# A sample group's attention queries: broadcast by matmul in PSUM against broadcast by DMA in SBUF, in a two-layer decoder step

## The chip, the cores and the metric

One Trainium2 chip, 8 cores, all with the same program on different data: each core holds one of the 8 prompt sequences and 16 of the 128 samples. The metric is the device time of the slowest core in microseconds.

## The reference, cut to what matters

```python
def mem_attend(u, k, v, w_q, w_o):
    b, t, d = u.shape
    q = jnp.einsum('btd,de->bte', u, w_q).reshape(b, t, MEM_HEADS, MEM_HEAD_DIM)
    s = jnp.einsum('bthd,bnhd->bhtn', q, k).astype(jnp.float32) * (MEM_HEAD_DIM ** -0.5)
    p = jax.nn.softmax(s, axis=-1).astype(v.dtype)
    o = jnp.einsum('bhtn,bnhd->bthd', p, v).reshape(b, t, d)
    return jnp.einsum('btd,de->bte', o, w_o)

for i in range(DEPTH):                      # DEPTH = 2; D_MODEL = 1024
    x = x + mixer_i(rmsnorm(x, g_mix[i]))   # 0: causal pooling, 1: gated short convolution
    x = x + mem_attend(rmsnorm(x, g_attn[i]), mem_k[i], mem_v[i], w_q[i], w_o[i])
    x = x + sq_relu_mlp(rmsnorm(x, g_ffn[i]), w_up[i], w_down[i])
```

The prompt group (8 sequences of 2048 tokens) attends to 256 memory tokens whose K and V are computed here. The sample group (128 samples of one new token) attends to cached K and V, 256 tokens for each sample and layer, which are read from DRAM: 1 MB of K and 1 MB of V for each sample and layer in fp32.

## The kernel before, in words

**Tiles.** A core has 2048 prompt tokens and 16 sample tokens, in five tiles of 416, 416, 416, 416 and 400 columns; the last holds 384 prompt tokens and the 16 samples. The residual `X` is kept transposed (8 chunks of 128 features by 2064 tokens, fp32) in SBUF for the whole program; `U3` beside it holds the normalised input in bf16 and then the attention output.

**Stages.** The pooling mixer (to about 100 us), attention and MLP of layer 0, the convolution mixer (from about 840 to 1030 us), attention and MLP of layer 1. `layer` is called once for each layer with the last two.

**Attention.** `layer` goes through the tiles in the order `seq = [0, 4, 1, 2, 3]`; step k is the tile `seq[k]`. Q for the first tile is made ahead (8 groups of 8 matmuls, each group in one PSUM bank, evacuated by ScalarE). In each step four heads follow one another. A head h consists of `S(k, h + 1)` (scores of the next head: 4 matmuls, two banks, exponentiated by ScalarE into `PT`), a share of the list `big`, `PVh(k, h)` (6 matmuls, three banks: the denominators, which ScalarE turns into reciprocals, and two outputs, which VectorE multiplies by them and writes into `U3` at L316) and a second share of `big`. `big` holds the Q groups of the next tile and the O groups of an earlier one (`Ogroup`: 8 matmuls that read all 8 chunks of the tile's `U3`, one bank, added to `X` by VectorE). The table `cut` says how many eighths of `big` come where. `norm_h` squares half a tile on ScalarE; `norm_t` sums the squares with 8 matmuls and writes the normalised tile with 8 VectorE operations (L312), in head 2 of each step.

**Samples.** While the prompt tiles go on, one sample after the other is attended to in 18 slots. A slot i does four things: `SE(i - 1)`, the exponential of the scores of sample i - 1 on ScalarE and its copy into the zero-padded `PZ`; `SB(i - 2)`, 4 matmuls of 512 columns with V, which accumulate in bank 7; `SDV(i)`, the two loads of V on POOL's queue; `SQB(i)`, two matmuls of 512 columns whose left operand selects row i of `QS`, so that q of sample i stands on all 128 partitions in banks 5 and 6; and `SA(i)`, in which VectorE multiplies the two K tiles with it, 8 operations of 256 columns with a running sum (L336), each followed by a read of the accumulator. Each half of `SA` is followed by `SDK`, which loads a K tile (512 KB) on SP's queue into the buffer that this half released; there are three K buffers, so the tile of the second half of sample i + 1 is issued in the middle of sample i. `sample_q(1)` makes `QS` (16 partitions by 1024, bf16) at the end of head 2 of step 0: 8 transposes of the last tile's Q (L292) and a ScalarE copy (L328). The slots stand in the list `slots` for the first 12 samples; one is among the O groups of the last tile, and the other five stand in the first MLP stages (`mid`).

**Order and waits.** There is no scheduler: each engine runs its instructions in program order, and `Prog.add` derives the semaphores from the byte ranges of reads and writes. `PSv` marks a whole bank, and as exclusive (`excl=True`): a read of a bank is tracked as a write, so two reads of a bank by one engine other than TensorE are ordered by a semaphore too. `nxt()` hands out PSUM banks in turn, `bank_ctr % bank_mod`; `bank_mod` is 5 during attention and the first MLP stages, since banks 5 and 6 hold the sample's q and bank 7 its output, and 8 later. `wrelease_spread` cuts the load that replaces `wq` into 8 pieces, of which `wspread_step(2)` issues two in each slot on POOL's queue.

**Lines.** L283 is the matmul helper, L287 and L292 those for transposes and mixed groups, L300 and L303 activations, L312 `scalar_tensor_tensor`, L316 `tensor_tensor`, L328 and L330 copies on ScalarE and VectorE, L336 the multiply with a sum, L343 every DMA.

Of the kernel before, what the change touches and what calls it, by code (L numbers as in the profile page):

```python
# [8 lines left out]
BF16 = mybir.dt.bfloat16  # L9
# [4 lines left out]
PE, ACT, DVE, POOL, SP = "pe", "act", "dve", "pool", "sp"  # L14
NCORES = 8
D = 1024
NCH = 8
SEQ = 2048
NS = 16
# [4 lines left out]
QDB = 1 << 28  # L24
# [108 lines left out]
def build_program():  # L133
    nc = bass.Bass("TRN2", target_bir_lowering=False)
# [34 lines left out]
    ncs_d = dout("ncs", [NS, 2, D])  # L169

    mn_d = nc.dram_tensor("mn", [128, NCH, NMEM], BF16, kind="Internal").ap()

    es = contextlib.ExitStack()
    MEM = es.enter_context(nc.sbuf_tensor("MEM", [128, MEM_BYTES // 2], BF16))
# [2 lines left out]
    def DV(ap):  # L177
        return V(ap, [])
# [53 lines left out]
    def sl(a, b):  # L232
        return slice(a, b)

    def PSv(bank, a, b, m=128):
        return V(PS[0:m, bank, a:b], [(PSB + bank * 2048, PSB + (bank + 1) * 2048)], excl=True)
# [6 lines left out]
    bank_mod = [7]  # L243

    def nxt():
        b = bank_ctr[0] % bank_mod[0]
        bank_ctr[0] += 1
        return b
# [3 lines left out]
    def palloc(dt, shape):  # L252
        t = T(top[0], dt, shape)
        top[0] += (t.nbytes + 63) // 64 * 64
        return t
# [12 lines left out]
    IDB = palloc(BF16, [128])  # L268
# [13 lines left out]
    def mm(out, lhsT, rhs, start, stop):  # L282
        P.add(PE, "c", lambda e, o=out.ap, l=lhsT.ap, r=rhs.ap: e.matmul(out=o, lhsT=l, rhs=r, start=start, stop=stop),  # L283
              [lhsT, rhs], [out])
# [9 lines left out]
    def act(out, in_, func, scale=1.0, bias=0.0):  # L294
        rd = [in_]
        sc = scale
        if isinstance(scale, V):
            rd.append(scale)
            sc = scale.ap
        P.add(ACT, "c", lambda e, o=out.ap, i=in_.ap: e.activation(out=o, in_=i, func=func, bias=bias, scale=sc), rd, [out])  # L300
# [25 lines left out]
    def cp(out, in_, eng=DVE):  # L326
        if eng == ACT:
            P.add(ACT, "c", lambda e, o=out.ap, i=in_.ap: e.copy(out=o, in_=i), [in_], [out])  # L328
        else:
            P.add(eng, "c", lambda e, o=out.ap, i=in_.ap: e.tensor_copy(out=o, in_=i), [in_], [out])  # L330
# [4 lines left out]
    def ttr(out, in0, in1, acc):  # L335
        P.add(DVE, "c", lambda e, o=out.ap, a=in0.ap, b=in1.ap, c=acc.ap: e.scalar_tensor_tensor(  # L336
            out=o, in0=a, scalar=1.0, in1=b, op0=ALU.mult, op1=ALU.mult, accum_out=c), [in0, in1], [out, acc])
# [4 lines left out]
    def dma(q, out, in_, chan, after=()):  # L342
        P.add(q, "d", lambda e, o=out.ap, i=in_.ap: e.dma_start(out=o, in_=i), [in_], [out], chan=chan, after=after)  # L343
# [485 lines left out]

    def layer(l, side=None, tail=None):  # L830
        fin = l == 1
        bank_mod[0] = 5
        s2 = Scratch2()
        SQ = s2.alloc(BF16, [NCH, TW])
        HB = [s2.alloc(BF16, [NCH, TW]) for _ in range(2)]
# [7 lines left out]
        assert so == ZOFF  # L843
        KS = [s2.alloc(F32, [D]) for _ in range(3)]
        VS = [s2.alloc(BF16, [2, 512]) for _ in range(4)]
        QS = s2.alloc(BF16, [D])
        PZ = [s2.alloc(BF16, [4, PZW]) for _ in range(2)]
        OSN = T(KS[0].off, F32, [512])
        Wq, Wo = W(f"wq{l}"), W(f"wo{l}")
        seq = [0, 4, 1, 2, 3]  # L850
# [3 lines left out]
        def norm_h(ti, half):  # L854
            c0, n, npmt, ns = TILES[ti]
            act(SQ(sl(half * 4, half * 4 + 4), sl(0, n)), X(sl(half * 4, half * 4 + 4), sl(c0, c0 + n)), AF.Square)
# [13 lines left out]
        def Ogroup(ti, ec):  # L870
            c0, n, npmt, ns = TILES[ti]
            bk = nxt()
            for kc in range(NCH):
                mm(PSv(bk, 0, n), Wo(kc, sl(ec * 128, (ec + 1) * 128)), U3(kc, sl(c0, c0 + n)), kc == 0, kc == NCH - 1)
            tt(X(ec, sl(c0, c0 + n)), PSv(bk, 0, n), X(ec, sl(c0, c0 + n)), ALU.add)
# [26 lines left out]
        def sample_q(k):  # L902
            npmt = TILES[seq[k]][2]
            bk = nxt()
            psb = PS[0:NS, bk, :].bitcast(BF16)
            iv = PSv(bk, 0, 1).ivs
            for c in range(NCH):
                tp(V(psb[:, c * 128:(c + 1) * 128], iv, True), HB[k % 2](c, sl(npmt, npmt + NS)), IDB())
            cp(QS(p=(0, NS)), V(psb, iv, True), eng=ACT)

        def SDK(i):
            if i < 2 * NS:
                dma(SP, KS[i % 3](), DV(ck_d[l, i // 2, (i % 2) * 128:(i % 2 + 1) * 128, :]), f"ks{i % 3}")

        def SQB(b):
            sel = V(IDB.ap[0:NS, b:b + 1].broadcast_to([NS, 128]), IDB(sl(b, b + 1)).ivs)
            for hf in range(2):
                mm(PSv(5 + hf, 0, 512), sel, QS(sl(hf * 512, (hf + 1) * 512), p=(0, NS)), True, True)

        def SDV(b):  # L920
            for hf in range(2):
# [3 lines left out]
        def SA(b):  # L925
            for ncx in range(2):
                ks = KS[(2 * b + ncx) % 3]
                for h in range(4):
                    a = sl(h * 256, (h + 1) * 256)
                    ttr(ks(a), ks(a), PSv(5 + h // 2, (h % 2) * 256, (h % 2 + 1) * 256),  # L930
                        SS(b, ncx * 2 + h // 2, sl(h % 2, h % 2 + 1)))
                SDK(2 * b + ncx + 3)

        def SE(b):
            act(PBC(sl(0, 4), sl(2 * b, 2 * b + 2)), SS(b), AF.Exp, scale=1.0 / 16.0)
# [11 lines left out]
        def slot():  # L947
            i = sctr[0]
            sctr[0] += 1
            if 0 <= i - 1 < NS:  # L950
                SE(i - 1)
            if 0 <= i - 2 < NS:
                SB(i - 2)
            if i < NS:
                SDV(i)
                SQB(i)
                SA(i)
            wspread_step(2)

# [25 lines left out]
        for ec in range(NCH):  # L985
            Qgroup(0, ec)
            if ec == 3:
                norm_t(seq[1], R_ATTN + l)
        slots = [(0, 3), (1, 0), (1, 1), (1, 3), (2, 0), (2, 2), (3, 0), (3, 1), (3, 3), (4, 0), (4, 1), (4, 3)]
        for k in range(5):  # L990
            big = []
            if k + 1 < 5:
                big += [lambda ec=ec: Qgroup(k + 1, ec) for ec in range(NCH)]
            if k > 0 and seq[k - 1] != 4:
                big += [lambda ec=ec: Ogroup(seq[k - 1], ec) for ec in range(NCH)]
            nb = len(big)
            cut = [0, 1, 2, 3, 4, 5, 6, 7, 8] if k else [0, 2, 4, 6, 7, 8, 8, 8, 8]
            nrm = (seq[k + 2], R_ATTN + l) if k + 2 < 5 else ((k - 3, R_FFN + l))
            S(k, 0)
            for h in range(4):  # L1000
                if h < 3:
                    S(k, h + 1)
                if h < 2:
                    norm_h(nrm[0], h)
                for f in big[nb * cut[2 * h] // 8: nb * cut[2 * h + 1] // 8]:
                    f()
                PVh(k, h)
                if h == 2:
                    norm_t(*nrm)
                for f in big[nb * cut[2 * h + 1] // 8: nb * cut[2 * h + 2] // 8]:  # L1010
                    f()
                if (k, h) == (0, 2):
                    sample_q(1)
                if (k, h) in slots:
                    slot()
            if k == 3:
                wrelease_spread(f"wq{l}")
# [295 lines left out]
```

How the kernel before makes its waits and increments, by code:

```python
    def emit(name, e):  # L1202
        known = {}
        for op in P.q[name]:
            for d in op.cwaits:
                key = ("e", d.eng)
                if known.get(key, 0) < d.val:
                    e.wait_ge(sems[d.eng], d.val)
                    known[key] = d.val
            for ch, val in op.dwaits:
                key = ("c", ch)
                if known.get(key, 0) < val:
                    e.wait_ge(chans[ch], val)
                    known[key] = val
            ins = op.fn(e)
            if op.kind == "d":
                ins.then_inc(chans[op.chan], 16)
            elif op.sig:
                ins.then_inc(sems[name], 1)
        if name == SP:
            for ch, cnt in P.chan_count.items():
                if known.get(("c", ch), 0) < cnt * 16:
                    e.wait_ge(chans[ch], cnt * 16)
```

## Time and profile before

| | before |
|---|---|
| three runs, median | 1682.01 us (1681.29 to 1682.10) |
| the profiled execution, its own time | 1683.78 us |
| its span, slowest core (core 7) | 1682.0 us |
| spans of the eight cores | 1675.8 to 1682.0 us |
| TensorE busy | 1625.3 us (97%) |
| VectorE, ScalarE, POOL busy | 886.9, 515.8 and 83.3 us |
| K loads of the samples, 64 of 512 KB, median to landing | 6.7 us |
| V loads of the samples, 64 of 256 KB, median to landing | 6.9 us |
| attention of layer 0, of layer 1 | about 115 to 285 us, 1020 to 1190 us |

In the profile a busy time counts the union of an engine's instructions, and matmuls overlap with the next one, so that the mean duration of one is longer than the time from one start to the next. The idle time before an instruction is put down to what it waited for last. PEld is the weight load, which overlaps the matmuls.

### The profile page before, as it was taken

The page shows a single profiled execution, that of the slowest core. Times are in us where ns is not written, and L with a number is a line of the kernel's source. Part 1 is how long each engine was busy: PE and PEld are TensorE (multiplying, and loading weights), DVE is VectorE, ACT ScalarE, POOL GpSimd, SP SyncE. Part 2 cuts the span into 40 slices and gives each one's busy share as a digit, 9 for nine tenths or more (in the row PEclk, how much of TensorE's full clock was granted, in tenths as well). Part 3 has the DMA queues.
Part 4 walks back from the last instruction along what each step waited for, and adds up shares of the span by engine and source line. Part 5 has one row for each costly group of instructions (what it writes and reads, how often), then busy time and mean ns, then how long its engine had stood idle before and what let it go on. Part 6 is the DMA issues. An engine that isn't in the chain of part 4 may idle for free.

```text
span 1682.0 us, 27775 instructions; the slowest of 8 cores (1675.8 to 1682.0 us)
## 1 busy us (share of the span) xinstructions
PE 1625.3 (97%) x9556; PEld 918.4 (55%) x9556; DVE 886.9 (53%) x1979; ACT 515.8 (31%) x996; POOL 83.3 (5%) x120
## 2 busy tenths in 40 slices
PE   5899999999999999999999999999999999999997
PEld 4754454555555555555555554544555555555565
DVE  4655667644433444455666573657654444444455
ACT  4765442312112211222222136443312111111244
POOL 1010011100000000000000000101100000000000
PEclk8999999999999999999999999999999999999999
DMA  9995658617506333306000067556813503303013
GB/s 243 195 180 100 141 106 177 106 35 114 87 13 112 65 67 51 51 2 100 1 1 1 1 94 140 120 138 134 168 26 55 86 12 51 51 1 51 10 74 120
DMA packets 68835, 137.97 MB, mean 82 GB/s; under 512 B 3918, under 2 KB 27598, under 8 KB 68684
## 3 DMA queue, kind: packets, MB, share of 16 engines
q0 software_dynamic: 50304, 76.44, 31.1%
q1 hardware_dynamic: 18396, 59.77, 10.4%
q8 instruction: 80, 1.31, 0.3%
q14 instruction: 55, 0.45, 0.1%
HBM read 199.25 MB, written 14.36 MB: 127 GB/s over the span
## 4 chain that ended last, share of the span: by engine, by line
PE 90%; DVE 3%; DMA 3%; ACT 2%; issue 1%; SPq 1%; DVEq 0%; ACTq 0%
PE PS L283 88%; DVE MEM L312 2%; DMA MEM<-ck 2%; PE PS L292 1%; DMA MEM<-mem 1%; PE PS L287 1%; ACT MEM L303 1%; SPq L343 1%; ACT MEM L300 1%; DVE MEM L336 1%; DVE MEM L316 0%; ACT MEM L328 0%; ACT PS L300 0%; DVE MEM L330 0%; DVEq L1208 0%
## 5 line engine op out<-in xcount | busy, mean ns | idle before, releaser
L283 PE MATMUL PS<-MEM 128*128 128x416 bf16 (+7 forms) x8900 | 1570.8, 338 | 47.2 <-DVE MEM L316 20.6
L283 PEld LDWEIGHTS PS<-MEM 128*128 128x128 bf16 (+4 forms) x8900 | 860.0, 99 | 746.5 <-issue 103.5
L316 DVE TENSOR_TENSOR MEM<-PS,MEM 128x416 f32<-128x416 f32 (+5 forms) x601 | 339.1, 583 | 330.4 <-PE PS L283 269.1
L300 ACT ACTIVATE MEM<-PS 128x416 f32<-128x416 f32 (+3 forms) x465 | 234.4, 515 | 654.9 <-PE PS L283 552.4
L316 DVE TENSOR_TENSOR MEM<-MEM 128x416 bf16<-128x416 f32 (+1 forms) x320 | 186.5, 588 | 256.7 <-ACT MEM L300 256.7
L312 DVE SCALAR_TENSOR_TENSOR MEM<-MEM 128x416 bf16<-128x416 f32 (+5 forms) x314 | 191.8, 659 | 100.4 <-ACT MEM L300 95.3
L300 ACT ACTIVATE MEM<-MEM 128x1 f32<-128x1 f32 (+7 forms) x201 | 125.1, 632 | 95.1 <-DVE MEM L316 77.5
L336 DVE SCALAR_TENSOR_TENSOR MEM<-MEM,PS 128x256 f32<-128x256 f32 x256 | 100.6, 419 | 33.6 <-DMA MEM<-ck 10.9
L328 ACT COPY MEM<-PS 128x512 f32<-128x512 f32 (+4 forms) x76 | 41.4, 547 | 177.1 <-PE PS L283 155.2
L328 ACT CAST MEM<-PS 128x416 bf16<-128x416 f32 (+3 forms) x101 | 51.8, 516 | 61.3 <-PE PS L283 53.0
L300 ACT ACTIVATE PS<-PS 128x416 f32<-128x416 f32 (+2 forms) x65 | 32.8, 504 | 122.0 <-PE PS L283 122.0
L343 POOL DMA_DIRECT2D MEM<-cv x64 | 45.0, 709 | 283.2 <-PE PS L283 282.8
L312 DVE SCALAR_TENSOR_TENSOR MEM<-PS,MEM 128x1024 f32<-128x1024 f32 (+2 forms) x20 | 25.6, 1281 | 26.0 <-ACT MEM L300 26.0
L287 PE MATMUL PS<-MEM 128*128 128x128 bf16 (+1 forms) x384 | 34.6, 249 | 1.1 <-issue 0.5
L292 PE MATMUL PS<-MEM 128*128 128x128 f32 (+8 forms) x272 | 33.7, 266 | 0.6 <-DVE MEM L312 0.5
L343 POOL DMA_DIRECT2D MEM<-w_down x22 | 14.0, 634 | 399.1 <-PE PS L283 347.5
L287 PEld LDWEIGHTS PS<-MEM 128*128 128x128 bf16 (+1 forms) x384 | 31.8, 119 | 1.6 <-issue 1.1
L292 PEld LDWEIGHTS PS<-MEM 128*128 128x128 f32 (+8 forms) x272 | 28.5, 131 | 7.4 <-issue 3.9
L303 ACT ACTIVATE MEM<-PS 128x1024 bf16<-128x1024 f32 (+2 forms) x20 | 20.4, 1018 | 34.5 <-PE PS L292 34.5
L303 ACT ACTIVATE MEM<-MEM 128x1024 bf16<-128x1024 f32 (+1 forms) x19 | 20.0, 1054 | 13.0 <-DMA MEM<-x 7.6
L330 DVE COPY MEM<-MEM 128x2 f32<-128x2 f32 (+2 forms) x120 | 16.1, 168 | 15.0 <-ACT MEM L300 14.8
L336 DVE DVE_READ_ACCUMULATOR MEM<-MEM,PS 128x1 f32 x256 | 21.2, 83 | 0.0
(26 smaller groups left out, 83.1 us busy)
## 6 DMA issues: line engine op xcount, KB each, us to landing
MEM<-ck SPq DMA_DIRECT2D x64, 512.0 KB, 6.7
MEM<-w_up POOLq DMA_DIRECT2D x8, 2048.0 KB, 16.5
MEM<-cv POOLq DMA_DIRECT2D x64, 256.0 KB, 6.9
MEM<-w_down POOLq DMA_DIRECT2D x6, 2048.0 KB, 16.3
MEM<-x SPq DMA_DIRECT2D x16, 512.0 KB, 14.3
y<-MEM SPq DMA_DIRECT2D x15, 512.0 KB, 2.6
MEM<-w_conv_in POOLq DMA_DIRECT2D x3, 2048.0 KB, 16.2
MEM<-w_kv POOLq DMA_DIRECT2D x4, 1024.0 KB, 25.0
```

Source lines behind the costliest of these rows:

```text
L283: P.add(PE, "c", lambda e, o=out.ap, l=lhsT.ap, r=rhs.ap: e.matmul(out=o, lhsT=l, rhs=r, start=start, stop=stop), [lhsT, rhs], [out])
L287: P.add(PE, "c", lambda e, o=out.ap, l=lhsT.ap, r=rhs.ap: e.matmul(out=o, lhsT=l, rhs=r, start=start, stop=stop, is_transpose=is_transpose ...
L292: P.add(PE, "c", lambda e, o=out.ap, i=in_.ap, d=ident.ap: e.transpose(out=o, in_=i, identity=d), [in_, ident], [out])
L300: P.add(ACT, "c", lambda e, o=out.ap, i=in_.ap: e.activation(out=o, in_=i, func=func, bias=bias, scale=sc), rd, [out])
L303: P.add(ACT, "c", lambda e, o=out.ap, i=in_.ap, c=acc.ap: e.activation(out=o, in_=i, func=func, bias=0.0, scale=1.0, accum_out=c), [in_], ...
L312: P.add(eng, "c", lambda e, o=out.ap, a=in0.ap, b=in1.ap: e.scalar_tensor_tensor(out=o, in0=a, scalar=sc, in1=b, op0=op0, op1=op1), rd, [out])
L316: P.add(eng, "c", lambda e, o=out.ap, a=in0.ap, b=in1.ap: e.tensor_tensor(out=o, in0=a, in1=b, op=op), [in0, in1], [out])
L328: P.add(ACT, "c", lambda e, o=out.ap, i=in_.ap: e.copy(out=o, in_=i), [in_], [out])
L330: P.add(eng, "c", lambda e, o=out.ap, i=in_.ap: e.tensor_copy(out=o, in_=i), [in_], [out])
L336: P.add(DVE, "c", lambda e, o=out.ap, a=in0.ap, b=in1.ap, c=acc.ap: e.scalar_tensor_tensor(out=o, in0=a, scalar=1.0, in1=b, op0=ALU.mult, ...
L343: P.add(q, "d", lambda e, o=out.ap, i=in_.ap: e.dma_start(out=o, in_=i), [in_], [out], chan=chan, after=after)
```

## The change

1. `SQB` is gone. `sample_q` writes `QS` to a DRAM tensor `qd`, and `SDQ(b)` reads row b of it back, broadcast to 128 partitions, into one of two SBUF buffers `QB` (bf16, 2 KB a partition; `QS` is the first of them). `SDQ(0)` and `SDQ(1)` follow the store, `SDQ(b + 2)` follows `SA(b)`. All of them are on SP's queue. `SA` multiplies with `QB` instead of banks 5 and 6.
2. `bank_mod` is 7 in `layer` instead of 5.
3. The O groups: before, all 8 of the previous tile stood behind the Q groups in steps 1, 3 and 4. Now four or eight stand ahead of the Q groups in every step: tile 0 in steps 1 and 2, tile 1 in steps 3 and 4, tile 2 in step 4, which has 12.
4. Four slots move, so that steps 1 to 4 have 3, 3, 3 and 2 samples instead of 3, 2, 3 and 3. In step 4 the two halves of the squares are made in heads 0 and 2 and `norm_t` comes in head 3.

```diff
-        bank_mod[0] = 5
+        bank_mod[0] = 7
...
-        QS = s2.alloc(BF16, [D])
+        QB = [s2.alloc(BF16, [D]) for _ in range(2)]
+        QS = QB[0]
...
             cp(QS(p=(0, NS)), V(psb, iv, True), eng=ACT)
+            dma(SP, V(qd_d[l], [(QDB + 8192 + l * 4096, QDB + 12288 + l * 4096)]), QS(p=(0, NS)), "qd")
+            for b in range(2):
+                SDQ(b)
...
-        def SQB(b):
-            sel = V(IDB.ap[0:NS, b:b + 1].broadcast_to([NS, 128]), IDB(sl(b, b + 1)).ivs)
-            for hf in range(2):
-                mm(PSv(5 + hf, 0, 512), sel, QS(sl(hf * 512, (hf + 1) * 512), p=(0, NS)), True, True)
+        def SDQ(b):
+            if b < NS:
+                dma(SP, QB[b % 2](), V(qd_d[l, b:b + 1, :].broadcast_to([128, D]),
+                                       [(QDB + 8192 + l * 4096, QDB + 12288 + l * 4096)]), f"qb{b % 2}")
...
-                    ttr(ks(a), ks(a), PSv(5 + h // 2, (h % 2) * 256, (h % 2 + 1) * 256),
+                    ttr(ks(a), ks(a), QB[b % 2](a),
                         SS(b, ncx * 2 + h // 2, sl(h % 2, h % 2 + 1)))
                 SDK(2 * b + ncx + 3)
+            SDQ(b + 2)
...
-                SQB(i)
                 SA(i)
...
-        slots = [(0, 3), (1, 0), (1, 1), (1, 3), (2, 0), (2, 2), (3, 0), (3, 1), (3, 3), (4, 0), (4, 1), (4, 3)]
+        slots = [(0, 3), (1, 0), (1, 2), (1, 3), (2, 1), (2, 2), (2, 3), (3, 1), (3, 2), (3, 3), (4, 1), (4, 2)]
...
-            if k > 0 and seq[k - 1] != 4:
-                big += [lambda ec=ec: Ogroup(seq[k - 1], ec) for ec in range(NCH)]
+            og = [[], [(0, 0)], [(0, 4)], [(1, 0)], [(1, 4), (2, 0), (2, 4)]][k]
+            big = [lambda t=t, ec=ec: Ogroup(t, ec) for t, e0 in og for ec in range(e0, e0 + 4)] + big
...
-                if h < 2:
-                    norm_h(nrm[0], h)
+                if h in ((0, 2) if k == 4 else (0, 1)):
+                    norm_h(nrm[0], h // 2 if k == 4 else h)
...
-                if h == 2:
+                if h == (3 if k == 4 else 2):
                     norm_t(*nrm)
```

## Rows read from the trace of the kernel before

**Rows 1.** The page, part 1: busy time, share of the span, instructions.

```profile
PE 1625.3 (97%) x9556; PEld 918.4 (55%) x9556; DVE 886.9 (53%) x1979; ACT 515.8 (31%) x996; POOL 83.3 (5%) x120
```

**Rows 2.** All cores: span and mean granted clock of TensorE.

```profile
core 1: 1675.8 us, clock 0.991
...
core 7: 1682.0 us, clock 0.987
```

**Rows 3.** Waits of TensorE, 100 to 330 us: total, times, longest.

```profile
PE PS L283 <- DVE MEM L316: 11.1, 6, 4.2
PE PS L283 <- ACT MEM L328: 0.5, 1, 0.5
```

**Rows 4.** The same, 1000 to 1240 us.

```profile
PE PS L283 <- DVE MEM L316: 9.5, 6, 2.7
```

**Rows 5.** Windows, core 7: length, busy by engine, then PEclk, DMA share, GB/s.

```profile
145.00:150.00 5.00, 5.00 (x22) 2.49 (x21) 2.13 (x12) 2.72 (x5) 0.00 (x0) 0.71 0.55 143
205.00:210.00 5.00, 3.62 (x13) 1.65 (x14) 1.62 (x6) 2.50 (x3) 0.00 (x0) 0.66 0.84 210
265.00:270.00 5.00, 4.62 (x14) 2.05 (x15) 5.00 (x10) 0.00 (x0) 1.73 (x3) 0.50 0.92 179
270.00:275.00 5.00, 5.00 (x25) 2.23 (x23) 3.54 (x9) 2.60 (x4) 0.14 (x1) 0.92 0.96 140
1045.00:1050.00 5.00, 5.00 (x21) 2.43 (x20) 2.74 (x14) 2.81 (x5) 0.00 (x0) 0.66 0.40 114
1105.00:1110.00 5.00, 3.38 (x11) 1.44 (x12) 1.86 (x8) 2.46 (x3) 0.00 (x0) 0.71 0.67 211
1165.00:1170.00 5.00, 5.00 (x21) 2.30 (x18) 5.00 (x10) 0.37 (x1) 0.54 (x1) 0.66 1.03 183
```

**Rows 6.** The same view of core 1, behind its wait at 204 us.

```profile
205.00:210.00 5.00, 5.00 (x31) 2.77 (x29) 0.56 (x2) 3.78 (x6) 0.00 (x0) 1.00 0.31 106
```

**Rows 7.** Groups by form, TensorE, 500 to 600 us (MLP): count, busy us, mean ns.

```profile
L283 PE MATMUL PS<-MEM 128*128 128x416 bf16 x391 | 70.2, 339 | 0.0
...
L283 PE MATMUL PS<-MEM 128*128 128x512 bf16 x40 | 9.4, 379 | 0.0
```

**Rows 8.** Timeline, 138 to 144 us: start, length, what, [idle before, releaser].

```profile
138.08 0.98 ACT L328 COPY MEM<-PS 16x1024 bf16<-16x1024 bf16 x1
138.36 4.59 DVE L312 SCALAR_TENSOR_TENSOR MEM<-MEM 128x416 bf16<-128x416 f32 x8 [0.99 <-ACT MEM L300]
...
139.21 1.67 PE L283 MATMUL PS<-MEM 16*128 16x512 bf16 x8 [0.53 <-ACT MEM L328]
...
142.87 1.08 DVE L316 TENSOR_TENSOR MEM<-PS,MEM 128x416 bf16<-128x416 f32 x2
...
143.59 16.66 PE L283 MATMUL PS<-MEM 128*128 128x384 bf16 x83 [2.71 <-DVE MEM L316]
```

**Rows 9.** The same view, inside a sample's multiplies at 296 us.

```profile
296.68 0.42 DVE L336 SCALAR_TENSOR_TENSOR MEM<-MEM,PS 128x256 f32<-128x256 f32 x1
...
297.03 0.42 DVE L336 SCALAR_TENSOR_TENSOR MEM<-MEM,PS 128x256 f32<-128x256 f32 x1
...
297.56 0.42 DVE L336 SCALAR_TENSOR_TENSOR MEM<-MEM,PS 128x256 f32<-128x256 f32 x1
```

**Rows 10.** The same view, a multiply in step 4 that waits for K.

```profile
262.89 0.42 DVE L336 SCALAR_TENSOR_TENSOR MEM<-MEM,PS 128x256 f32<-128x256 f32 x1 [4.10 <-DMA MEM<-ck]
```

**Rows 11.** DMA, 245 to 275 us: a queue's packets, MB, share; an issue's median landing.

```profile
q1 hardware_dynamic: 864, 3.15, 29.4%
...
MEM<-ck SPq DMA_DIRECT2D x6, 512.0 KB, 7.2
```

**Rows 12.** DMA issues of the whole span: KB each, median us to landing.

```profile
MEM<-gv SPq DMA_DIRECT2D x1, 512.0 KB, 3.7
...
ys<-MEM SPq DMA_DIRECT2D x1, 64.0 KB, 1.9
npp<-MEM SPq DMA_DIRECT2D x1, 60.0 KB, 6.3
```

More of the change, by code:

```diff
@@ L171, in build_program @@
     mn_d = nc.dram_tensor("mn", [128, NCH, NMEM], BF16, kind="Internal").ap()
+    qd_d = nc.dram_tensor("qd", [2, NS, D], BF16, kind="Internal").ap()
     es = contextlib.ExitStack()
```

## The prediction, made before the change was run

> **What bounds the kernel now.** I read the page first. TensorE is busy 1625.3 of 1682.0 us [rows 1], so the time can only fall if TensorE gets less to do, idles less, or runs at a higher clock. The list of cores [rows 2] says which of these varies: core 1 ends 6.2 us before core 7 and was granted 0.991 against 0.987 of the full clock. The waits of TensorE give the places: in layer 0's attention stage it waits 11.1 us for VectorE's evacuations (L316) in six waits and 0.5 us for one ScalarE copy [rows 3]; in layer 1's, 9.5 us in six [rows 4], and the same 0.5 us. The MLP, the longest part, has none. Then the windows of 5 us: behind the long waits the granted clock is 0.50 to 0.71 in five-microsecond windows in which TensorE is mostly busy [rows 5], so each long wait is paid a second time at the lower of its two levels (1.2 against 2.4 GHz). What that costs is (1 - clock) x 5 us: 1.45 + 1.7 + 2.5 + 0.4 in layer 0, 1.7 + 1.45 + 1.7 in layer 1, that is 6.05 and 4.85 us. On core 1 the stretch behind the wait at 204 us stayed at 1.00 [rows 6], which is why the cores differ.
>
> So what TensorE loses around attention on core 7 is 11.6 + 6.05 = 17.65 us in layer 0 and 10.0 + 4.85 = 14.85 us in layer 1. ScalarE, POOL and the queues matter here only through VectorE.
>
> **Part 1, the selector matmuls go.** SQB issued two 512-column matmuls for each of 16 samples in 2 layers: 64. They ran in TensorE's stream and nothing covers them. In the MLP 391 matmuls of 416 columns take 70.2 us, 0.180 each, which is 0.221 for 512 columns; the 512-column ones there take 9.4/40 = 0.235 [rows 7]. I take 0.22: **14.1 us** (ends 14.1 and 15.0). The 0.53 us wait of the first SQB for the copy of q [rows 8] goes too; it is among the stalls.
>
> **Part 2, VectorE's sample work gets shorter.** SA is 8 multiplies with a sum. Their starts are 0.35 us apart where the bank of q changes and 0.53 apart where two read the same bank [rows 9]: the program marks a read of a bank as exclusive, so the second waits for the first on VectorE's own semaphore. q in SBUF has no such mark, so I take 0.35 for all: 2.8 us a sample instead of 3.5. Below, 2.8 may be too dear by nothing that a row shows; above, it stays 3.5. This lies beside matmuls, so it is worth nothing in itself; it shortens what the banks must bridge.
>
> **Part 3, seven banks and spread O groups.** An allocation returns to the same bank after 7 instead of 5. With the costs of [rows 7], a group is 8 x 0.18 = 1.44 us and a head's scores and PV 10 x 0.18 = 1.8 us. A head with three groups takes 8 banks in 6.1 us (7.0 with a sample's four V matmuls), so 7 banks let TensorE run some 5.5 us ahead; 5 banks at four groups a head gave about 4. The longest VectorE block is one norm, 8 operations in 4.59 us, then two of 0.54 [rows 8], often with SA behind it. VectorE's work in tile step 1, 2 or 3 of the change: 3 samples x 3.0 + 4 O evacuations x 0.59 + 4 x 1.08 + 4.59 = 20.3 us, against TensorE's 12 x 1.44 + 4 x 1.8 + 3 x 0.94 = 27.3. In step 4: 2 x 3.0 + 12 x 0.59 + 4.32 + 4.59 = 22.0 against 17.3 + 7.2 + 1.9 = 26.4. Before, step 4 had three samples and eight O groups: 3 x 3.7 + 4.7 + 4.32 + 4.59 = 24.7 against 11.5 + 7.2 + 2.8 + 1.3 = 22.8, VectorE-bound; the 4.17 us wait there is this, with a K tile that came 4.10 us late [rows 10]. And step 4's norm now stands behind the last head's PV, so that its 8 statistics matmuls and two groups (4.3 us) lie between that head and the O groups of tile 3 that read it. I take all waits from step 1's end on as gone, but 1.0 us a layer for what I can't see.
>
> **What stays: the passage from step 0 to step 1.** It is late for another reason. VectorE does the norm from 138.36 to 142.95 and then the two PV evacuations of head 3, until 143.95; TensorE stood still 2.71 us for their bank [rows 8]. After the change TensorE does S(1,0), S(1,1) without the 0.53 + 0.44 us of SQB, until 138.7 + 2 x 0.65 = 140.0. Then comes not a Q group but O(0,0), which reads the very U3 chunks 6 and 7 that these evacuations write. It gets through six of eight matmuls, to 141.1, and waits until 143.9: 2.8 us. So the stall stays about as long; only the work done before it is larger. I take 2.8 us and one clock dip of 1.7 (the 0.66 windows of [rows 5]) in each layer. What stays in a layer is 2.8 + 1.7 + 1.0 = 5.5 us.
>
> **Part 4, the new transfers.** q goes from SBUF to DRAM and back to 128 partitions before SA(0) can start. The copy of q ends at 139.06; VectorE is free for SA(0) at 143.95, so 4.9 us are covered by the norm. Two legs, on a DMA that is nearly idle just then: a 64 KB store landed in 1.9 us and a broadcast row of 512 KB in 3.7 [rows 12]; here it is 32 KB and 256 KB, so 1.9 + 3.7 = 5.6 us at most by these, 3.8 if the second leg is like the first. I take 0 to 0.7 us late and count 0, as O(0,0)'s bank isn't wanted again for 4 us. The other end is the 6.3 us of the early npp store [rows 12] for each leg: 12.6, so 7.7 us late in each layer. If the cover were gone it would be the whole trip. [...] SP waits meanwhile for the copy and the store; behind it stand only the first two rows and the refill of K, which waits for SA(0) anyway.
>
> For all other samples the row is issued a whole sample ahead, behind the K tiles that SP issues for the same release, so SP waits for nothing new. Each is 128 packets of 2 KB. A packet on that queue costs 0.294 x 16 x 30 / 864 = 0.163 us [rows 11] at 3.6 KB, so a row takes 0.7 (by bytes) to 1.3 us (by packets) of all 16 engines, hidden unless it delays K. There is the danger: a K tile lands in 7.2 us in the crowded stretch [rows 11], and neighbouring samples are now 7.0 us apart in six pairs a layer (9 before with four groups a head). So VectorE will wait 1 to 1.5 us for K there; it has 4 to 7 us of slack in a step and TensorE 5.5 us of banks. I price it at the 1.0 us above. POOL's own order is as before but for the weight pieces (two a slot): step 4 issues four instead of six, the slot among tile 3's O groups two as before, and the rest goes out behind those groups; they are first read two MLP halves of 8 x 1.44 us later, 23 us against a landing of some 6 to 9 us, so I price that at nothing. The second q buffer moves PZ up by 2 KB, which changes only which early tile its clearing waits for: nothing.
>
> **The sum.** 14.1 + (17.65 - 5.5) + (14.85 - 5.5) = 35.6 us off the profiled execution's 1683.8 us (span 1682.0) gives 1648.2. The three runs' median, 1682.0, is 1.8 below that execution, so I forecast **1646.4 us**. About 0.2% (3.4 us) is what a measurement of this kernel can tell from no change.
>
> **Rivals.**
> 1. *Cleaner than I think*: the stall at step 1 brings no dip, as on core 1 [rows 6], and nothing else stays: 2 x 2.7 us more, 1641. For it: the K slack. Against: the slowest of eight cores counts, and core 7 had a dip behind every wait of 2.6 us or more.
> 2. *K tiles late.* With the rows' traffic K lands 3 us or more too late in one or two pairs a layer, as it did at 262.89 [rows 10]. One such costs 2.7 us of stall and a dip of 1.7; two a layer, 4 x 4.4 = 17.6: 1664. For it: samples in neighbouring heads of steps 2 and 3, DMA share 0.92 to 1.03 in the windows at 265 and 1165 [rows 5]. Against: the wq0 successor's pieces no longer meet three samples in step 4.
> 3. *The round trip is late.* 7.7 us at SA(0) in each layer, of which TensorE's banks cover little: + 15, 1661. Against: the DMA engines are idle at 140.
> 4. *Slower.* The same mechanism as 2, but everywhere: the row of each sample pushes K so far back that all six pairs a layer stall. It decides from 35.6/12 = 3.0 us a pair; at the measured wait of 4.17 with a dip of 1.7 it costs 12 x 5.9 = 70: 1717. Against: a row is at most 1.3 us of engine time where a K tile lands in 7.2.
> 5. *Nothing*: what TensorE is spared in part 1 it idles for VectorE, which is the real bound of attention, in the same places. Against: 20.3 against 27.3 us.
>
> **How the numbers follow.** Forecast 0.52, rival 1 0.12, rival 2 0.20, rival 3 0.07, rival 4 0.05, rival 5 0.04. The likeliest case alone is 1642 to 1653 (stall at step 1 with or without a dip, K waits 0 to 3 us a layer, SQB 14.1 to 15.0). The range, 1640 to 1665, takes in rivals 1 to 3 and leaves out 4 and 5 and the tails. Faster: the first four, 0.91; same: rival 5, 0.04; slower: rival 4, 0.05.
>
> **What would show it.** Right: no 16x512 matmuls; the multiplies 0.35 us apart; TensorE's waits for L316 at 5 to 7 us in all instead of 20.6, nearly all at the start of step 1, each with O(0,0) behind it; the clock at 1.00 at 205, 265 and 1105; SA(0) starting right behind the two evacuations. Wrong: multiplies still 0.53 apart (part 2); VectorE waiting for the q row at SA(0) (rival 3); waits for ck above the present 10.9 us, with TensorE idle behind them (rivals 2 and 4); a new wait at the passages 2 to 3 or 4 to the last O groups. The forecast falls if the time is above 1655 without late K, or if the step-1 stall is gone.

## The result, and the profile after

The changed kernel takes 1658.7 us (median; 1657.8 to 1659.0) against 1682.05 before: a ratio of 0.9858, 95% interval 0.9844 to 0.9873. It is faster by 23 us, or 1.4%; 1646.4 had been forecast, 12 us less than was measured, inside the range of 1640 to 1665. The profiled execution took 1658.7 us, its slowest core (core 2) 1657.2; the eight spans lie between 1643.1 and 1657.2, further apart than before. Here and below, executions in which half of the cores ran at a lower granted clock are left out of every time and ratio, which puts some medians up to 1.8 us below those that the recorded expectations quote.

First the waits of TensorE on the slowest core, layer 0 (100 to 330 us), which answer to [rows 3]; columns: total, times, longest.

```profile
PE PS L284 <- DMA MEM<-w_down: 12.1, 1, 12.1
PE PS L284 <- DVE MEM L317: 4.1, 4, 2.1
PE PS L284 <- ACT MEM L301: 0.3, 1, 0.3
```

The same view of layer 1 (1000 to 1230 us), which answers to [rows 4].

```profile
PE PS L284 <- DVE MEM L317: 4.1, 4, 1.9
PE PS L284 <- DMA MEM<-w_down: 4.0, 1, 4.0
PE PS L284 <- ACT MEM L301: 0.4, 1, 0.4
```

(All lines are one higher: L284 is the matmul, L317 `tensor_tensor`.) The waits for VectorE fell from 20.6 to 8.2 us. In their place stands one that was not there: at 291 us of layer 0 TensorE stands still for 12.1 us until the weights of the first down-projection have landed, and it does so for 4.0 us in layer 1. All eight cores wait there, 3.7 to 12.1 us in layer 0 and 1.0 to 6.3 in layer 1.

The second view is the timeline of POOL on core 2, where these weights are issued: start, length, what, and the idle time before it with its releaser.

```profile
241.88 0.57 POOL L344 DMA_DIRECT2D MEM<-w_down  x1
256.95 0.55 POOL L344 DMA_DIRECT2D MEM<-w_down  x1 [14.49 <-PE PS L284]
...
262.54 0.54 POOL L344 DMA_DIRECT2D MEM<-w_down  x1 [3.61 <-DMA MEM<-w_down]
272.83 0.54 POOL L344 DMA_DIRECT2D MEM<-w_down  x1 [9.74 <-PE PS L284]
...
277.21 0.54 POOL L344 DMA_DIRECT2D MEM<-w_down  x1 [2.39 <-DMA MEM<-w_down]
288.32 0.54 POOL L344 DMA_DIRECT2D MEM<-w_down  x1 [10.56 <-DMA MEM<-w_down]
293.75 0.53 POOL L344 DMA_DIRECT2D MEM<-w_down  x1 [4.89 <-DMA MEM<-w_down]
298.00 0.53 POOL L344 DMA_DIRECT2D MEM<-w_down  x1 [3.71 <-DMA MEM<-w_down]
```

Eight pieces need 56 us from first issue to last, since each waits for the one before it to land. (Two of the waits are put down to TensorE; but the first piece lands 14.5 us after its issue, at 256.4, and the third 9.7 us after its own, at 272.2, and the next one follows each time.) The wait is in the code, not in the data: all pieces have one semaphore (`chan`), and `Prog.add` makes a DMA that writes where an earlier one of this channel wrote wait for everything issued on the channel so far. Before, the same chain ran from 249.4 to 294.7 us on this core, 45 us, its last piece landed at 302.7, and TensorE reached the down-projection after it, at about 310 us (the first of its groups is evacuated at 311.64). Now the chain starts 7.5 us earlier and is 11 us longer, so that its last piece lands at 303.3, just when it did before; but TensorE gets there at 291 us, some 19 sooner.

Third, the passage from step 0 to step 1 on core 2, in the timeline; it answers to [rows 8].

```profile
136.67 0.98 ACT L329 COPY MEM<-PS 16x1024 bf16<-16x1024 bf16 x1
...
138.91 1.21 PE L284 MATMUL PS<-MEM 128*128 128x416 bf16 x6 [0.34 <-ACT MEM L301]
...
141.46 1.08 DVE L317 TENSOR_TENSOR MEM<-PS,MEM 128x416 bf16<-128x416 f32 x2
142.18 0.34 PE L284 MATMUL PS<-MEM 128*128 128x416 bf16 x1 [2.06 <-DVE MEM L317]
142.68 7.51 PE L284 MATMUL PS<-MEM 128*128 128x416 bf16 x33 [0.16 <-DVE MEM L317]
...
143.64 0.43 DVE L337 SCALAR_TENSOR_TENSOR MEM<-MEM 128x256 f32<-128x256 f32 x1 [1.10 <-DMA MEM<-qd]
...
143.99 0.42 DVE L337 SCALAR_TENSOR_TENSOR MEM<-MEM 128x256 f32<-128x256 f32 x1
...
144.34 0.42 DVE L337 SCALAR_TENSOR_TENSOR MEM<-MEM 128x256 f32<-128x256 f32 x1
```

Six of the eight matmuls of O(0,0) run, then one, then the rest: TensorE is waiting for the two U3 chunks that VectorE writes, one after the other, in the middle of a group whose bank it already has. That is 2.06 + 0.16 = 2.22 us; with the 0.34 for ScalarE ahead of the group the passage costs 2.56. The q row comes 1.10 us after VectorE is free, and the multiplies then stand 0.35 us apart, all of them.

The windows of core 2 give the clock (last but two) behind the waits, as in [rows 5].

```profile
140.00:145.00 5.00, 2.78 (x12) 1.41 (x12) 3.90 (x12) 2.63 (x4) 0.00 (x0) 0.85 0.34 107
145.00:150.00 5.00, 5.00 (x25) 2.55 (x24) 4.83 (x21) 1.30 (x4) 0.00 (x0) 0.81 0.59 180
205.00:210.00 5.00, 4.96 (x29) 2.80 (x30) 3.56 (x7) 3.41 (x5) 0.00 (x0) 1.00 1.00 199
265.00:270.00 5.00, 5.00 (x31) 2.77 (x29) 2.97 (x7) 1.54 (x3) 0.00 (x0) 1.00 1.01 195
300.00:305.00 5.00, 1.57 (x5) 0.74 (x6) 0.00 (x0) 0.00 (x0) 1.39 (x2) 0.50 1.00 146
305.00:310.00 5.00, 5.00 (x23) 2.53 (x22) 1.38 (x3) 0.00 (x0) 0.00 (x0) 0.77 0.71 116
1105.00:1110.00 5.00, 5.00 (x30) 2.79 (x29) 3.23 (x17) 2.88 (x7) 0.86 (x2) 1.00 0.83 150
1187.00:1192.00 5.00, 4.79 (x18) 2.25 (x19) 0.61 (x2) 0.00 (x0) 0.00 (x0) 0.66 1.13 170
```

The old dips at 205, 265 and 1105 us are gone, the one behind the passage remains in layer 0 (0.75 + 0.95 = 1.7 us), and each wait for w_down brings one of its own: 1.57 x 0.5 = 0.8 and 1.15 us, and 1.7 us in layer 1. So by the trace that wait costs 16.1 + 3.65 = 19.7 us on core 2.

VectorE's waits for K rose from 10.9 to 18.2 us between the two slowest cores. TensorE stood behind them for only 1.53 us at 205, 0.34 at 233 and 0.81 at 1069.

### The profile page after: what moved, and what is told of

It is laid out like the page before. It is cut to its first block, busy times and chain, and to the rows that moved or that the text cites. A ratio compares the mean times of both kernels' runs of the same rounds, so it can differ in the third digit from the quotient of the medians.

```text
span 1657.2 us, 27574 instructions; the slowest of 8 cores (1643.1 to 1657.2 us)
## 1 busy us (share of the span) xinstructions
PE 1598.9 (96%) x9492; PEld 918.1 (55%) x9492; DVE 875.2 (53%) x1979; ACT 516.1 (31%) x996; POOL 83.3 (5%) x120
## 4 chain that ended last, share of the span: by engine, by line
PE 86%; DMA 7%; DVE 2%; ACT 2%; issue 2%; SPq 1%; DVEq 0%; ACTq 0%; POOL 0%; POOLq 0%
PE PS L284 84%; DMA MEM<-w_down 5%; DVE MEM L313 2%; PE PS L293 1%; DMA MEM<-mem 1%; PE PS L288 1%; DMA MEM<-ck 1%; ACT MEM L304 1%; ACT MEM L301 1%; SPq L344 1%; DVE MEM L337 0%; DMA MEM<-qd 0%; DVE MEM L317 0%; ACT PS L301 0%; DVE MEM L331 0%
## 5 line engine op out<-in xcount | busy, mean ns | idle before, releaser
L284 PE MATMUL PS<-MEM 128*128 128x416 bf16 (+5 forms) x8836 | 1543.1, 337 | 49.0 <-DVE MEM L313 16.3
L284 PEld LDWEIGHTS PS<-MEM 128*128 128x128 bf16 (+2 forms) x8836 | 858.7, 99 | 721.8 <-issue 67.5
L317 DVE TENSOR_TENSOR MEM<-PS,MEM 128x416 f32<-128x416 f32 (+5 forms) x601 | 339.0, 583 | 332.4 <-PE PS L284 288.5
L317 DVE TENSOR_TENSOR MEM<-MEM 128x416 bf16<-128x416 f32 (+1 forms) x320 | 186.4, 588 | 256.6 <-ACT MEM L301 256.6
L337 DVE SCALAR_TENSOR_TENSOR MEM<-MEM 128x256 f32<-128x256 f32 x256 | 91.5, 420 | 22.1 <-DMA MEM<-ck 18.2
L344 POOL DMA_DIRECT2D MEM<-w_down x22 | 13.9, 633 | 406.6 <-PE PS L284 317.3
L337 DVE DVE_READ_ACCUMULATOR MEM<-MEM 128x1 f32 x256 | 20.8, 81 | 0.0
L344 POOL DMA_DIRECT2D MEM<-w_up x8 | 7.0, 877 | 256.9 <-PE PS L284 256.9
## 6 DMA issues: line engine op xcount, KB each, us to landing
MEM<-x SPq DMA_DIRECT2D x16, 512.0 KB, 13.9
```

What stands on the lines that cost most here:

```text
L317: P.add(eng, "c", lambda e, o=out.ap, a=in0.ap, b=in1.ap: e.tensor_tensor(out=o, in0=a, in1=b, op=op), [in0, in1], [out])
```

## The experiments

Times are medians; each ratio is to the kernel before, run beside it on the same chip. Not all runs shared a chip (the kernel before took 1681.7 to 1684.1 us on them), so a difference between two runs is given by the ratios too where the two disagree. "Rows" are the transfers of q to 128 partitions.

| run | edit | us | ratio (95%) |
|---|---|---|---|
| changed kernel | | 1658.7 | 0.9858 (0.9844 to 0.9873) |
| own_chan | changed, pieces not chained | 1645.6 | 0.9781 (0.9750 to 0.9811) |
| early | changed, two pieces earlier | 1657.3 | 0.9857 (0.9834 to 0.9880) |
| no_rows | changed, 4 of 32 rows | 1647.7 | 0.9789 (0.9771 to 0.9806) |
| chan_q_first | own_chan, Q ahead of O in step 1 | 1639.3 | 0.9740 (0.9725 to 0.9755) |
| selector_once | before, 2 of 32 selector matmuls a layer | 1673.5 | 0.9940 (0.9918 to 0.9961) |
| rows_only | before, q by DMA | 1685.3 | 1.0009 (0.9997 to 1.0021) |
| rows_banks | rows_only, 7 banks | 1672.6 | 0.9938 (0.9914 to 0.9961) |
| before_chan | before, pieces not chained | 1687.3 | 1.0020 (1.0009 to 1.0031) |
| chan_q_first_no_rows | chan_q_first, 4 of 32 rows | 1634.9 | 0.9708 (0.9687 to 0.9729) |
| rows_only_no_rows | rows_only, 4 of 32 rows | 1668.9 | 0.9906 (0.9890 to 0.9922) |
| chan_q_first_early | chan_q_first, two pieces earlier | 1642.0 | 0.9750 (0.9727 to 0.9772) |
| chan_q_first_late | chan_q_first, pieces later | 1636.5 | 0.9727 (0.9713 to 0.9741) |

(selector_once keeps the pair of sample 0 in each layer, so 60 of 64 matmuls go, not 62 as its expectation says; the rows are counted over both layers.)

**own_chan: is it the chain or the bytes?**

```diff
-            wspread.append(lambda kc=kc: dma(POOL, tile(kc), DV(wsrc[nm][:, kc, :]), chan))
+            wspread.append(lambda kc=kc: dma(POOL, tile(kc), DV(wsrc[nm][:, kc, :]), f"{chan}p{kc}"))
```

> The changed kernel with one edit: each of the eight pieces of the weight load that replaces wq has a semaphore of its own, so that a piece no longer waits for the one before it to land (4 waits of 3.6 to 10.6 us stand on POOL's queue between the pieces in the changed kernel's layer 0). Theory A (the pieces run one behind the other, and this chain ends too late for the first down-projection): the 12.1 and 4.0 us for which TensorE waits for w_down on the slowest core go, with the clock dip behind the long one; 1658.9 - 16 to 18 = 1641 to 1643 us, which is what was forecast but for this. Theory B (the DMA engines are full there, share 0.92 over 238 to 300 us, so the bytes themselves are late): the pieces land together but no earlier, the wait for w_down stays above 6 us in layer 0, and the time at 1652 us or more.

Measured: 1645.6, with executions from 1641.7 to 1652.5; the median is 2.6 us above the span given for theory A and under that of B. The timeline of POOL on its slowest core (core 4), same columns as above:

```profile
249.34 1.12 POOL L344 DMA_DIRECT2D MEM<-w_down  x2
...
256.20 1.10 POOL L344 DMA_DIRECT2D MEM<-w_down  x2
...
269.39 2.16 POOL L344 DMA_DIRECT2D MEM<-w_down  x4
```

Eight pieces go out within 22 us, and the wait for w_down is 0.8 us on two cores and nothing on the rest. A piece now lands only 12.4 to 22.3 us after its issue (3.7 to 14.5 in the changed kernel), but they fly together: the last lands at 292.2, 43 us after the first issue, against 61 in the changed kernel. The bytes fit, though the DMA share over 238 to 300 us is 1.00 on this core (in the changed kernel it was 0.79 on core 2, not the 0.92 that the expectation gives). On its two slowest cores TensorE still waits 6.8 and 7.0 us for L317, and 1.7 for V on one of them. Those waits stand behind late K and V at 197 to 241 us, before the first piece is issued at 246 or 249, so they aren't the price of the unchained pieces.

**early: start the chain sooner.** After `wrelease_spread` at the end of step 3 stands one more `wspread_step(2)`.

> The changed kernel with one edit: two pieces more are issued at the end of tile step 3, still one behind the other on one semaphore. Theory A: the chain of eight pieces starts earlier by what lies between the end of step 3 and the first slot of step 4 (one head, 6 us) at most, and ends 5 to 8 us earlier; TensorE's wait for w_down falls from 12.1 to 4 to 7 us in layer 0 and from 4.0 to nothing in layer 1; 1648 to 1652 us. Theory B (bytes): starting two pieces earlier moves bytes into an equally full stretch and delays K; the waits for ck grow by about what w_down gains, 1655 us or more.

Measured: 1657.3, outside A's span and inside B's. The wait for w_down fell as A said (4.4 us or less on all cores), but TensorE got a new one, for V, of up to 7.2 us. The waits of TensorE in layer 0 on its slowest core:

```profile
PE PS L284 <- DVE MEM L317: 5.7, 4, 2.2
PE PS L284 <- DMA MEM<-w_down: 4.4, 1, 4.4
PE PS L284 <- DMA MEM<-cv: 3.1, 1, 3.1
```

POOL issues in order: a chained piece that waits for its predecessor holds up the V loads behind it. So the chain costs in two ways, and shifting it only changes one for the other. VectorE's waits for K didn't grow (15.2 us against 18.2), so the reason given for B was wrong, though its time came.

**no_rows: do the rows lengthen the chain?** `SDQ` loads for `b < 2` only; samples 2 to 15 of each layer are scored with another sample's q.

> The changed kernel, but only the first two q rows of each layer are read back; samples 2 to 15 are scored with the row of sample 0 or 1, so the sample outputs differ. It takes 28 transfers of 256 KB away and nothing else. If the rows' traffic is what made the weight pieces late (they cost 0.7 to 1.3 us of all DMA engines each, some 6 of them while the chain runs), the wait for w_down falls by 4 to 8 us in layer 0 and the time to 1648 to 1654 us, and K lands in 6.7 us again instead of 7.4. If the chain's own order is enough (pieces that start later because step 4 has two slots), it stays within 2 us of 1658.9.

Measured: 1647.7, 11 us faster, and the wait for w_down at most 4.8 us in layer 0. K didn't come back to 6.7 us: its median landing is 7.2. So both causes are needed for the full loss: with the chain the rows cost 11 us, without it 4 to 5 (chan_q_first_no_rows below); and without the rows the chain still leaves those 4.8 us of wait.

**chan_q_first: data or bank at the passage?**

```diff
+            og_ = [lambda t=t, ec=ec: Ogroup(t, ec) for t, e0 in og for ec in range(e0, e0 + 4)]
+            big = big[:2] + og_ + big[2:] if k == 1 else og_ + big
```

> own_chan, and in tile step 1 two Q groups ahead of the four O groups of tile 0. It tests the reason given for the stall at the passage from step 0 to step 1 (0.34 + 2.06 + 0.16 us in layer 0 of the changed kernel): O(0,0) reads the U3 chunks that VectorE writes behind its norm. If so, one Q group runs in the stall, and with seven banks the next use of the bank of PV(0,3) comes after it: 1.4 us of matmuls are done in it, the stall falls from 2.6 to 0.5 to 1.2 us a layer, and the dip behind it mostly goes: 2.5 to 6 us below own_chan. If the bank and not the data is what TensorE waits for, the stall stays at 2.1 us or more and the time within 1 us of own_chan.

Measured: 1639.3, 6.2 us below own_chan and just past the span. The waits of TensorE in layer 0, slowest core (core 5):

```profile
PE PS L284 <- DVE MEM L317: 5.0, 3, 2.9
PE PS L284 <- DVE MEM L313: 0.9, 4, 0.2
PE PS L284 <- ACT MEM L301: 0.2, 1, 0.2
```

The stall of 2.56 us became four waits of 0.23 us, in which TensorE follows the norm chunk by chunk, one of 0.27 and the 0.24 for ScalarE: 1.4 us in all. It was the data. What is left in L317 is late K on some cores, in layer 0 only: on core 5, K is 3.65 us late at 202 us and 4.96 at 233, and TensorE then waits 1.85 and 2.85 us. Both stand before the first piece, which goes out at 245.

**selector_once: what were the matmuls worth?**

```diff
-                SQB(i)
+                if i == 0:
+                    SQB(i)
```

> The kernel before, in which SQB runs for sample 0 of each layer alone; banks 5 and 6 keep that q and all 16 samples are scored with it, so the sample outputs differ. It takes 62 of the 64 selector matmuls away and changes no bank, no slot and no transfer. If they were bare TensorE time (theory), 62 x 0.22 = 13.6 us go, less what the old order gives back as longer waits for VectorE in step 4 (2 to 4 us on the slowest core): 1669 to 1673 us. If attention was bound by VectorE (rival 5 of the prediction) TensorE's waits for L316 grow by as much as the matmuls took, and the time stays above 1678.

Measured: 1673.5, 10.2 us less than the kernel before beside it: just above the span. But not for the reason given. A pair of selector matmuls costs more than 2 x 0.22 us, and more is given back. The cost shows in the first MLP stages, where a slot comes every 8 groups and POOL's V loads mark the period. Before, core 0:

```profile
1204.56 1.50 POOL L343 DMA_DIRECT2D MEM<-cv  x2 [5.75 <-PE PS L283]
1217.33 1.40 POOL L343 DMA_DIRECT2D MEM<-cv  x2 [11.27 <-PE PS L283]
```

and in selector_once, core 7:

```profile
303.31 1.40 POOL L343 DMA_DIRECT2D MEM<-cv  x2 [4.25 <-PE PS L283]
315.43 1.40 POOL L343 DMA_DIRECT2D MEM<-cv  x2 [10.72 <-PE PS L283]
```

12.77 against 12.12: 0.65 us a pair, 0.325 each, so 60 cost 19.5 us. The page agrees: TensorE is busy 1605.5 us instead of 1625.3, 19.8 less. Its waits grew from 20.8 to 26.8 us on core 0, which gives 6 of them back; the theory had 2 to 4. (1.4 of the 6 are a wait for w_down, which the kernel before does not have: the reader comes sooner here too, with no rows at all.) That leaves 13.5 where 10.3 were gained between the two spans of core 0 (1679.2 and 1668.9); the longer waits bring longer dips (mean clock 0.987 against 0.988), but the 3 us weren't taken apart.

**rows_only: the DMA path alone.** Before with `qd`, `QB` and `SDQ` of the change, and nothing else of it.

> The kernel before with the q rows by DMA and without SQB, but with five banks, the old slots and the old O groups. Against selector_once it adds the rows' traffic and makes VectorE's sample 2.8 us instead of 3.5. Theory: the shorter SA is worth 1 to 3 us (the waits in steps 2 to 4 shrink), the traffic costs 0 to 4 us by later K tiles and weight pieces: 1666 to 1672 us. If the rows' traffic by itself is what delays the weight pieces, a wait for w_down of 3 us or more shows here already; if it takes the new slots too, none or under 2 us shows.

Measured: 1685.3, a ratio of 1.0009: a clear miss. All of the 20.8 us that TensorE was spared is given back. The wait for w_down is 1.0 us at most in layer 0 and 2.5 in layer 1: the old order hides the late pieces. Its waits on the slowest core, 130 to 320 us:

```profile
PE PS L284 <- DVE MEM L317: 9.3, 5, 2.8
PE PS L284 <- DMA MEM<-cv: 8.5, 4, 4.3
```

V is what comes late, as in early: in the POOL timeline of this core one piece is issued at 247.32 us, lands after 18.5 us, and the V loads behind its successor go out at 266.92.

**rows_only_no_rows: is it the traffic?**

> rows_only, but only the first two q rows of each layer are read back, so the sample outputs differ. rows_only came to 1686.6 with TensorE waiting 8.5 and 7.3 us for V (cv) on its slowest core, where selector_once, without rows, came to 1673.6 and had none. Theory: the rows' traffic lengthens the landing of the weight pieces, and V stands behind them on POOL's queue; without it the waits for cv go and the kernel comes to selector_once less the shorter SA: 1666 to 1672 us. If it is something else that the DMA path brought (the trip at SA(0), the SP queue's order), it stays at 1680 or more.

Measured: 1668.9, inside the span. With everything of the DMA path in place but 28 of the 32 rows, the waits for V are nothing to 3.6 us in layer 0, where they had been 3.6 to 8.5. So the rows' traffic costs 16 to 17 us in the old order (1685.3 - 1668.9, or 1.03% by the ratios), and V is where most of it shows. That the chain carries it to V is read from the POOL timeline; the old order with rows and unchained pieces was not run.

**rows_banks: banks against spreading.** rows_only with `bank_mod[0] = 7`.

> rows_only with seven rotating banks, still with the old slots and O groups. Theory: the banks are what takes most of the old waits away, the two of 2.65 us at the passage from step 2 to 3 and the 0.6 ones; with the Q groups ahead in step 1 the passage from step 0 to 1 is short too. TensorE waits for L316 3 to 5 us a layer on the slowest core, most in step 4, which still has three samples and no Q groups. 1648 to 1656 us, with a wait for w_down up to 8 us in layer 0. If the spreading of the O groups is what removes the waits, it stays above 1660.

Measured: 1672.6; a miss in the time, a hit for the banks. The waits for L317 in layer 0 fell from 9.3 to 12.2 us to 2.5 to 6.8, as expected, but V costs 5.9 to 12.3 us there. The banks are worth 12 to 13 us (1685.3 - 1672.6, or 0.71% by the ratios). The step from here to the changed kernel, slots and O groups, is worth another 13.5 to 14 us: in the changed kernel no core waits for V at all, though the rows are the same. Which of the moved slots does it (by the two lists there are five, not four) wasn't taken apart; step 4, where the pieces go out, has two samples instead of three and four more O groups.

**before_chan: own_chan's edit on the kernel before.**

> The kernel before with a semaphore of its own for each weight piece, the edit of own_chan. There TensorE never waited for w_down, so if the chain of pieces bound only the changed kernel, nothing moves: 1680 to 1683 us. If own_chan gained by something else (a less blocked POOL queue, V earlier), some of its 13 us show here, 1678 or less.

Measured: 1687.3, slower by 0.2% (interval 0.1 to 0.3) and above the span. The chain bound only the changed kernel. VectorE's waits for K are 17.1 us instead of 10.9 on the slowest core, and up to 19.4 instead of 12.2; the long wait at 263 us was there before, one of 3.00 us (core 1) or 4.21 (core 2) at 287 is new. So the pieces crowd K there.

**chan_q_first_no_rows: what the rows still cost.**

> chan_q_first, but only the first two q rows of each layer are read back, so the sample outputs differ. With the pieces no longer chained, it prices what the rows' traffic still costs. Theory: little, since K, V and pieces now have slack and TensorE waits for DMA 0.7 to 1.5 us in two cores only; the remaining waits for L317 in layer 0 (up to 5.0 us on one core, late K) shrink by half: 1634 to 1638 us against 1639.3. If the traffic costs by itself as much as no_rows showed against the changed kernel (11 us), it would come to 1628.

Measured: 1634.9, 4.4 us less, or 0.32% by the ratios, whose intervals just overlap; 11 had hung on the rows with the chain. TensorE's waits in layer 0 are 1.3 to 1.8 us in all on every core.

**chan_q_first_early and chan_q_first_late: where should unchained pieces go?** The first adds `wspread_step(2)` at the end of step 3; the second makes the `wspread_step(2)` of each slot `wspread_step(1)`.

> chan_q_first, and two pieces more are issued at the end of tile step 3. In the run named early the same edit with chained pieces came to 1657.3, since a piece that waits for the one before holds up the V loads behind it on POOL's queue. With unchained pieces nothing is held up: the last piece lands 6 us earlier, the waits for w_down of 0.7 and 1.5 us go, and the time is 1637 to 1640 us. If the bytes themselves crowd K there, VectorE's waits for ck grow above 20 us and the time is 1641 or more.

> chan_q_first, and each slot issues one weight piece instead of two; the remaining five go out together behind the O groups of the last tile. chan_q_first_early showed the opposite edit to make VectorE wait 27.1 us for K instead of 19.5 and to cost 4.5 us. If unchained pieces are harmful only by crowding K and V in step 4, moving them out of it helps: waits for ck 15 to 19 us, TensorE's waits for L317 in layer 0 under 2 us on all cores, 1636 to 1639 us. If five pieces at once are too late for the first down-projection, a wait for w_down of 2 us or more comes back and the time is 1640 or more.

Measured: 1642.0 for early (1639.4 to 1645.6), a miss: no wait for w_down is left, but VectorE waits 27.1 us for K. And 1636.5 for late, inside its span: VectorE waits 16.4 us for K, and no core waits for w_down. But the totals for K are not the pieces' doing alone. K is late at about 170, 200 and 230 us on nearly every core of chan_q_first and of both variants, and the first piece goes out at 225 to 245. What the edit can change comes behind it: from 240 us on, layer 0's waits for K are at most 1.4 us a core in chan_q_first, 1.1 to 4.2 in early and at most 1.6 in late. So two pieces more at that place do crowd K, and issuing fewer than chan_q_first does gains nothing there.

In time none of the three is shown to differ: the ratios are 0.9750, 0.9740 and 0.9727, and all their intervals overlap. On late's slowest core one wait of 4.0 us for L317 is left, at 207 us, where VectorE had waited 4.2 us for K before any piece was out; on the others they stayed under the 2 us expected.

## Why the prediction was right, and where it was wrong

The range held and the sign was right; the middle was off by 12 us. That the range held was in part luck: it reached to 1665 for rivals 2 and 3, and neither is what happened. Late K cost TensorE 2.7 us on core 2, not 17.6, and the late round trip 1.2, not 15. By the prediction's own sign the forecast falls: the time is above 1655, and not for late K. By its own steps:

**Part 1** was mis-sized. "I take 0.22: 14.1 us (ends 14.1 and 15.0)" for 64 matmuls; they cost 0.325 each, 20.8 us. The rows of the MLP's 512-column matmuls were the wrong neighbours: those have 128 rows of weights like everything around them, and the selector matmuls have 16, with one column repeated 128 times. Which of the two costs was not tried.

**Part 2** was right: 0.35 us between all multiplies. A single multiply takes 420 ns with q in SBUF against 419 with q in PSUM, so it isn't the place of the operand that counts; and in selector_once, where the banks are no longer rewritten but keep their exclusive mark, the starts still alternate between 0.35 and 0.53. That it is the mark, and not the second read of one bank, is argued from the code; no run takes the mark away alone.

**Part 3** was right in size. Outside w_down, core 2 waits 4.4 us in layer 0 and 4.5 in layer 1, with 1.7 us of dip in layer 0: 10.6 us for both against 5.5 x 2 = 11.0 forecast. Two misses cancel in that: layer 1 has no dip (1.7 less), and the waits behind the passage are 1.9 and 2.0 us instead of 1.0 a layer. The passage was forecast with 2.8 us, its place and its cause; it has 2.56, and chan_q_first shows the cause.

**Part 4** held nearly for the round trip: 1.1 us late in layer 0 and 2.3 in layer 1 against "0 to 0.7". In layer 0 TensorE ran on, as said; in layer 1 the row came at 1038.30, and at 1041.81 TensorE had waited 1.2 us for VectorE, a wait that layer 0 does not have. The trip took from the end of the copy at 137.65 to 143.64, 6.0 us: the store landed 1.6 us after its issue at 137.75, the first row was issued at 139.80 and landed in 3.7. The Trainium skill (DMA: Bandwidth & Descriptors, Anatomy of one DMA) gives a transfer that POOL issues a fixed cost of about 2.0 us. By that figure two would be an estimated 4 us; these two, issued by SP, took 1.6 + 3.7 = 5.3.

**The step that failed** is one sentence of Part 4: the pieces "are first read two MLP halves of 8 x 1.44 us later, 23 us against a landing of some 6 to 9 us, so I price that at nothing". That takes one piece's landing for that of eight. The trace of before had both things that were needed: waits of POOL for w_down between the pieces, and code that gives them one channel. Eight times 6 to 9 us is 48 to 72. The last two pieces were meant to go out 23 us ahead of their reader; they went out at 293.75 and 298.00, after it had come at 291. The chain itself ended no later than before; it is the reader that came 19 us sooner, which is what the change was for. The trace prices it at 19.7 us on core 2. Own_chan, which takes the chain away, gives back 13 us: the slowest core is then another one, with 8.7 us of waits behind late K and V. Rival 2 named the same traffic, but with K as its victim and VectorE between; the victims were the weights in the changed kernel and V in rows_only, rows_banks and early, all on POOL's queue, and TensorE directly.

So the sum with the measured terms is 20.8 + (17.65 - 6.1) + (14.85 - 4.5) - 19.7 = 23.0 us, against 24.8 between the two slowest spans; the rest, 1.8, lies within what cores differ by. Two errors of opposite sign, + 6.7 and - 19.7, make up the 12 to 13 us: with Part 1 as small as it was forecast, the time would have come out near 1665, at the end of the range.

What stays open: why the rows slow the pieces, when their own bytes are few. The first piece lands late without them too (8.6 to 13.9 us in no_rows, 8.8 to 15.5 in the changed kernel, in layer 0); over the eight cores they add on average 1.4 to 1.6 us to each of the first three pieces and 2.8 to the fifth, and the chain from first issue to last takes 44 to 50 us without them and 49 to 57 with them. That V is a victim of the queue's order is read from the timelines of early and rows_only; how the DMA engines share their time between the two queues was not tried.

## What to carry to other kernels

A load cut into pieces to be gentle is a chain if the pieces share a semaphore: price it as the number of pieces times their landing in that stretch (8 x 7.1 us here), and ask when its first link can start and when its reader comes, above all if the change lets the reader come sooner. Everything behind such a wait on an in-order queue is late with it. And an edit that removes engine time can be worth nothing (rows_only) until the order around it is changed too: measure each part in the kernel it will live in.

## What the runs showed of the hardware that was not expected

The selector matmuls, 16 rows of weights between matmuls of 128, cost more than their columns: 0.325 us for 512 columns, where the 4 of each slot with V cost (12.12 - 8 x 1.41)/4 = 0.21 each, a group of the MLP taking 1.41 us from one evacuation to the next. In the trace of before (core 0) PEld stands idle for 0.41 us ahead of the pair's weight loads and for 0.42 ahead of the one behind them, in both layers; why was not tested.

A broadcast of 2 KB to 128 partitions is not a cheap transfer: its median landing is 7.3 us over the span, as long as that of a K tile with twice the bytes. The first two of layer 0, with the queue to themselves, landed in 3.7 and 4.7; the others go out behind K tiles, so part of the 7.3 may be their wait for those.

```profile
MEM<-ck SPq DMA_DIRECT2D x64, 512.0 KB, 7.4
...
MEM<-qd SPq DMA_DIRECT2D x32, 256.0 KB, 7.3
```

Pieces in flight together each land late (12.4 to 22.3 us on own_chan's core 4), and yet the eighth lands 43 us after the first issue instead of 61.
